# Sparse stages: u by features ahead of v, and the pooling's running sums as shifted additions on GpSimd

## The reference, cut to what matters

```python
POOL_WINDOWS = (2, 4, 8, 16)
def pool_mixer(u, w_pool, pool_scale):
    ug = u.reshape(B, S, N_POOL_GROUPS, POOL_GROUP)          # 4 groups of 128 features
    cs = jnp.cumsum(ug.astype(jnp.float32), axis=1)
    for g, w in enumerate(POOL_WINDOWS):
        c = cs[:, :, g]
        lagged = jnp.pad(c, ((0, 0), (w, 0), (0, 0)))[:, :S]
        cnt = jnp.minimum(t + 1, w).astype(jnp.float32)[None, :, None]
        outs.append((c - lagged) / cnt - ug[:, :, g].astype(jnp.float32))
    d = jnp.stack(outs, axis=2).astype(u.dtype)
    y = jnp.einsum('bsgc,gcd->bsgd', d, w_pool)
    return y.reshape(B, S, POOL_WIDTH) * pool_scale
```

## Time and profile before

| what | value |
| --- | --- |
| median of 3 runs | 1811.44 us (1811.19 to 1811.59) |
| profiled execution | 1811.9 us, of which the span of the profile is 1810.1 us |
| busy in the span | PE 1798.3 us (99%), DVE 1312.2 (72%), ACT 1052.0 (58%), POOL 237.4 (13%) |
| granted clock of PE | 0.999 of full on average |
| the two sparse stages' middles | from about 1256 and from about 1536 us on, the same instructions at the same distances |

### The profile page before, as it was taken

The page is one execution under the profiler, slowest core; times in us unless marked ns, Lnnn a source line. Parts: engine busy times, 40 slices in busy tenths (PEclk is TensorE's granted clock), DMA queues, the critical chain, the costliest instruction groups (busy, mean ns, idle before and its releaser), DMA issues.

```text
span 1810.1 us, 26703 instructions
## 1 busy us (share of the span) xinstructions
PE 1798.3 (99%) x10311; PEld 1546.9 (85%) x10311; DVE 1312.2 (72%) x1714; ACT 1052.0 (58%) x1524; POOL 237.4 (13%) x259
## 2 busy tenths in 40 slices
PE   9999999999999999999999999999999999999998
PEld 7888899788888888889987888889888889888887
DVE  7767778876766776677688677667887667797665
ACT  7555546755655565455476665555775555675443
POOL 2010122110000011003021000002100111301110
PEclk9999999999999999999999999999999999999999
DMA  9686663462765567666345456555447664645662
GB/s 337 219 297 208 172 191 106 140 221 93 252 193 183 163 219 254 228 169 220 118 139 198 136 189 210 188 177 186 154 146 226 190 198 157 230 136 187 196 191 71
DMA packets 226815, 338.96 MB, mean 187 GB/s; under 512 B 22566, under 2 KB 170176, under 8 KB 226432
## 3 DMA queue, kind: packets, MB, share of 16 engines
q1 hardware_dynamic: 219200, 308.11, 52.5%
q0 software_dynamic: 7488, 29.14, 4.8%
HBM read 336.18 MB, written 1.05 MB: 186 GB/s over the span
## 4 chain that ended last, share of the span: by engine, by line
PE 95%; DVE 2%; DMA 1%; ACT 1%; SPq 0%; issue 0%; POOL 0%; DVEq 0%; ACTq 0%
PE ps L1809 92%; PE ps L1814 3%; DVE wlo L1195 1%; DMA raw<-ffn_w_down 1%; DVE xn L1195 1%; ACT whi L742 0%; DVE xs L1203 0%; DVE ahl L1195 0%; SPq L537 0%; POOL region L564 0%; SPq L549 0%; ACT xn L742 0%; DVE region L1195 0%; SPq L541 0%; ACT ahl L742 0%
## 5 line engine op out<-in xcount | busy, mean ns | idle before, releaser
L1195 DVE TENSOR_TENSOR wlo<-raw,whi 128x1024 fp32r<-128x1024 f32 (+2 forms) x452 | 560.7, 1241 | 172.3 <-ACT whi L742 137.2
L742 ACT ACTIVATE whi<-raw 128x1024 fp32r<-128x1024 f32 (+2 forms) x452 | 475.7, 1052 | 74.7 <-PE ps L1809 28.2
L1809 PE MATMUL ps<-ahl,whi 128*128 128x512 f32 (+1 forms) x1824 | 402.7, 355 | 0.6 <-ACT whi L742 0.6
L1809 PEld LDWEIGHTS ps<-ahl,whi 128*128 128x128 f32 x1824 | 320.9, 189 | 47.4 <-ACT whi L742 1.0
L742 ACT ACTIVATE region<-ps 128x512 f32<-128x512 f32 (+2 forms) x268 | 155.9, 582 | 272.9 <-PE ps L1809 220.2
L1809 PE MATMUL ps<-whi,ahl 128*128 128x512 f32 (+2 forms) x944 | 299.0, 385 | 0.5 <-ACT whi L742 0.5
L1809 PE MATMUL ps<-ahl,wlo 128*128 128x256 f32 x1520 | 244.4, 283 | 0.0
L1809 PEld LDWEIGHTS ps<-ahl,wlo 128*128 128x128 f32 x1520 | 214.8, 191 | 6.4
L1809 PEld LDWEIGHTS ps<-whi,ahl 128*128 128x128 f32 x944 | 174.2, 188 | 34.7 <-ACT region L742 1.6
L1195 DVE TENSOR_TENSOR mlo<-raw,mhi 128x1024 fp32r<-128x1024 f32 (+2 forms) x132 | 163.3, 1237 | 44.8 <-ACT mhi L742 35.4
L1809 PE MATMUL ps<-whi,hhi 128*128 128x512 f32 x472 | 185.7, 393 | 0.0
(11 more groups left out here) (176 smaller groups left out, 2349.1 us busy)
## 6 DMA issues: line engine op xcount, KB each, us to landing
raw<-w_ff SPq DMA_DIRECT2D x64, 1024.0 KB, 5.4
raw<-ffn_w_down SPq DMA_DIRECT2D x44, 1024.0 KB, 5.0
raw<-ffn_w_up SPq DMA_DIRECT2D x40, 1024.0 KB, 5.7
raw<-ffn_w_gate SPq DMA_DIRECT2D x39, 1024.0 KB, 5.3
raw<-w_in SPq DMA_DIRECT2D x34, 1024.0 KB, 5.4
raw<-w_out SPq DMA_DIRECT2D x16, 1024.0 KB, 4.9
raw<-xa_wk SPq DMA_DIRECT2D x8, 1024.0 KB, 5.1
raw<-xa_wv SPq DMA_DIRECT2D x8, 1024.0 KB, 5.0
```

Of the source, the lines that this page charges most:

```text
L742: e.activation(o, i, f, **kw).then_inc(*act.did(*names))
L1195: e.tensor_tensor(o, a, b, op).then_inc(*dve.did(*names))
L1809: m = e.matmul(o, l, r, start=start, stop=stop)
```

## The change

Per sparse stage:

- u is multiplied the other way round (`up`: features on the partitions, tokens as 256 columns), in two pieces of 256 features, ahead of v instead of behind it. It goes to PSUM banks 0 and 1, and v to banks 2 and 3, where u was. It is no longer scaled by ACT's per-partition scale; `turn_scales` on PE and `scales` on ACT make the roots as a row `R2S`, and POOL multiplies u by it.
- POOL adds shifted copies of u along the row (window 2, then 4, 8, 16 from one another), with 16 cleared elements ahead of each row; it corrects the first 16 tokens with the small constant `c_fix`, which takes the place of `c_pool`. ACT scales the four sums by 1/w in place, POOL subtracts u (`lagged`), which gives `DT`.
- PE's products with the matrix and ACT's copies of them go. PE's `pooled(0)` moves behind `out_part(0, 0)`, next to `pooled(1)`, and both wait for both `lagged`.
- The names in `take` swap u and v; the pieces' places in the queues stay.

```diff
-            for tag, c0, n in (("q", 512, 512), ("k", 1024, 512), ("v", 1536, 512), ("u", 0, 512)):
+            for tag, c0 in (("q", 512), ("k", 1024), ("u", 0), ("v", 1536)):
                 for c in range(2):
-                    item(s, tag, rows(wi, 4 * c, 4 * c + 4, c0, c0 + n), 4, n)
+                    if tag == "u":
+                        item(s, tag, rows(wi, 0, 8, 256 * c, 256 * c + 256), 8, 256)
+                    else:
+                        item(s, tag, rows(wi, 4 * c, 4 * c + 4, c0, c0 + 512), 4, 512)
...
+        UA, SB = [x.rearrange("p (g n) -> p g n", g=4) for x in (XN[:, 576:1664], R[:, 8704:9792])]
+        SCV = R[:, 4352:5168].rearrange("p (g n) -> p g n", g=3)
+        SUMS = (SB[:, 0, 16:272], SCV[:, 0, 16:272], SB[:, 2, 16:272], SCV[:, 2, 16:272])
... (gpsimd, sparse)
-                e.dma_start(PM, A["c_pool"]).then_inc(*region_in.did(("pool", l)))
+                e.dma_start(R[:, 9792:9856], A["c_fix"]).then_inc(*region_in.did(("pool", l)))
...
                 q.wait_ge(*pe.at("a_turned", s, 1, 1))
+                for v in (UA, SB, SCV):
+                    q.wait_ge(*pool.last())
+                    e.memset(v[:, :, 0:16], 0.0).then_inc(*pool.did())
                 q.wait_ge(*act.at("iq_rest", l, 1))
                 rope(iqh[:, :, 0:9, :], 9)
...
                 rope(kn.rearrange("p (m h d) -> p m h d", m=2, h=8), 8, ("k_rope", l))
+                for c in range(2):
+                    q.wait_ge(*act.at("u", l, c))
+                    u = UA[:, 2 * c:2 * c + 2, 16:272]
+                    tt(u, u, bm(R2S, 2), ALU.mult)
+                tt(SB[:, :, 16:272], UA[:, :, 16:272], UA[:, :, 15:271], ALU.add)
+                tt(SCV[:, :, 16:272], SB[:, 1:4, 16:272], SB[:, 1:4, 14:270], ALU.add)
+                tt(SB[:, 2:4, 16:272], SCV[:, 1:3, 16:272], SCV[:, 1:3, 12:268], ALU.add)
+                tt(SCV[:, 2, 16:272], SB[:, 3, 16:272], SB[:, 3, 8:264], ALU.add)
+                q.wait_ge(*region_in.at("pool", l))
+                for a, v in enumerate((SB, SCV)):
+                    tt(v[:, 0::2, 16:32], v[:, 0::2, 16:32], FIX[:, a], ALU.mult, ("sums", l, a))
+                q.wait_ge(*dve.at("score", l, 1))
+                for a, v in enumerate((SB, SCV)):
+                    q.wait_ge(*act.at("means", l, a + 2))
+                    tt(DTV[:, a::2, :], v[:, 0::2, 16:272], UA[:, a::2, 16:272], ALU.subtract, ("lagged", l, a))
... (scalar, sparse)
                 natural((2, 3), qn, "q")
+                scales(s)
                 heads(iqT, 4, "iqT")
...
                 heads(sqT, 2, "sqT")
-                take(s, "v", 1)
+                take(s, "u", 1)
+                pool_input(0)
                 heads(skT, 2, "skT")
-                take(s, "u", 0)
-                natural((0, 1), V, "v")
+                take(s, "v", 0)
+                pool_input(1)
                 exps("s", l, 0, 128, sP, 1.0)
                 exps("s", l, 1, 128, sP, 1.0)
-                take(s, "u", 1)
+                take(s, "v", 1)
                 take(s, "w_out2", 0)
-                natural((2, 3), U, "u")
+                natural((2, 3), V, "v")
                 turned(0)
                 turned(1)
-                means(0)
                 halves(s + 0.5, 0, 1, SVALUE[0])
-                means(1)
+                means()
                 pooled(0)
                 exps("s", l, 2, 256, sP, 1.0)
                 pooled(1)
...
+                def means():
+                    for g in (0, 2, 1, 3):
+                        q.wait_ge(*pool.at("sums", l, g % 2))
+                        put(SUMS[g], SUMS[g], ACT.Copy, ("means", l, g), scale=1.0 / POOL_WINDOWS[g])
... (tensor, sparse)
                 natural(s, "q", (2, 3), 512, ("q", l))
+                turn_scales(s)
...
-                natural_part(s, "v", 0, (0, 1), 512)
+                up(s, "u", 0, 0, ("u", l, 0))
...
-                natural_part(s, "v", 1, (0, 1), 512, ("v", l))
+                up(s, "u", 1, 1, ("u", l, 1))
...
                 scores(1)
-                natural_part(s, "u", 0, (2, 3), 512)
-                natural_part(s, "u", 1, (2, 3), 512, ("u", l))
+                natural_part(s, "v", 0, (2, 3), 512)
+                natural_part(s, "v", 1, (2, 3), 512, ("v", l))
...
+                q.wait_ge(*act.at("u", l, 1))
+                scores(3)
                 q.wait_ge(*act.at("v", l))
-                scores(3)
-                q.wait_ge(*act.at("u", l))
-                q.wait_ge(*region_in.at("pool", l))
-                for a in range(2):
-                    if a:
-                        values(0)
-                        values(1)
-                        q.wait_ge(*dve.at("s_shift", l, 2, 1))
-                    for g in (2 * a, 2 * a + 1):
-                        (two products of U with PM for each group: means)
+                values(0)
+                values(1)
                 def pooled(a):
-                    q.wait_ge(*act.at("means", l, a))
+                    q.wait_ge(*pool.at("lagged", l, 1))
...
-                pooled(0)
                 q.wait_ge(*dve.at("a", s + 0.5, 0, 1))
                 out_part(0, 0, first=True)
+                pooled(0)
                 pooled(1)
```

More of the change, by code:

```diff
@@ L124, in constants @@
     ).astype(np.float32)
-    pm = []
-    for w in POOL_WINDOWS:
-        cnt = np.minimum(t + 1, w)[:, None]
-        m = np.where((dist >= 0) & (dist < w), 1.0 / cnt, 0.0) - np.eye(T)
-        m = m.T
-        pm.append(np.concatenate([m[0:128, :], m[128:256, 128:256]], axis=1))
-    pool = np.concatenate(pm, axis=1).astype(np.float32)
-    return {"c_small": small, "c_decay": decay, "c_pool": pool}
+    fix = [[w / np.minimum(np.arange(16) + 1, w) for w in POOL_WINDOWS[a::2]] for a in range(2)]
+    fix = np.broadcast_to(np.asarray(fix).reshape(1, 64), (128, 64)).astype(np.float32)
+    return {"c_small": small, "c_decay": decay, "c_fix": np.ascontiguousarray(fix)}
 def bc(ap, n):
@@ L333, in build @@
         R2F, R2H, R2M = [R[:, c:c + 256] for c in (9216, 3840, 7168)]
-        R2 = {"ffn": R2F, "relu": R2F, "hybrid": R2H, "memory": R2M}
+        R2S = XN[:, 1664:1920]
+        R2 = {"ffn": R2F, "relu": R2F, "hybrid": R2H, "memory": R2M, "sparse": R2S}
         R2V = R2F.unsqueeze(1).broadcast_to([128, 2, 256])
@@ L437, in build @@
         V = R[:, 3328:4352]
-        U = R[:, 4352:5376]
+        UA, SB = [x.rearrange("p (g n) -> p g n", g=4) for x in (XN[:, 576:1664], R[:, 8704:9792])]
+        SCV = R[:, 4352:5168].rearrange("p (g n) -> p g n", g=3)
+        FIX = R[:, 9792:9856].rearrange("p (a g n) -> p a g n", a=2, g=2)
+        SUMS = (SB[:, 0, 16:272], SCV[:, 0, 16:272], SB[:, 2, 16:272], SCV[:, 2, 16:272])
         ikT = R[:, 5376:5632]
@@ L446, in build @@
         DT = R[:, 11136:12160]
+        DTV = DT.rearrange("p (g n) -> p g n", g=4)
         sP = [R[:, 1024 * i:1024 * i + 1024].rearrange("p (h n) -> p h n", h=4) for i in range(2)]
@@ L454, in build @@
         SBANK, STURN, SVALUE = (4, 6, 6, 0), ((4,), (5,), (2, 3), (2, 3)), (4, 4, 0, 1)
-        MEANBANK, POOLBANK = (3, 6), (2, 3)
+        POOLBANK = (2, 3)
         cosv = COS.rearrange("p (m j) -> p m j", m=2)
@@ L1134, in sparse @@
                 index(0)
-                take(s, "v", 0)
+                take(s, "u", 0)
                 natural((0, 1), kn, "k")
@@ L1139, in sparse, with pool_input @@
                 heads(sqT, 2, "sqT")
-                take(s, "v", 1)
+                take(s, "u", 1)
+                def pool_input(c):
+                    q.wait_ge(*pe.at("u", l, c))
+                    put(UA[:, 2 * c:2 * c + 2, 16:272], PS[:, c, :].rearrange("p (g n) -> p g n", g=2), ACT.Copy, ("u", l, c))
+                pool_input(0)
                 heads(skT, 2, "skT")
-                take(s, "u", 0)
-                natural((0, 1), V, "v")
+                take(s, "v", 0)
+                pool_input(1)
                 exps("s", l, 0, 128, sP, 1.0)
                 exps("s", l, 1, 128, sP, 1.0)
-                take(s, "u", 1)
+                take(s, "v", 1)
                 take(s, "w_out2", 0)
-                natural((2, 3), U, "u")
+                natural((2, 3), V, "v")
                 turned(0)
                 turned(1)
-                def means(a):
-                    q.wait_ge(*pe.at("means", l, a))
-                    put(DT[:, a * 512:a * 512 + 512], PS[:, MEANBANK[a], :], ACT.Copy, ("means", l, a))
+                def means():
+                    for g in (0, 2, 1, 3):
+                        q.wait_ge(*pool.at("sums", l, g % 2))
+                        put(SUMS[g], SUMS[g], ACT.Copy, ("means", l, g), scale=1.0 / POOL_WINDOWS[g])
                 def pooled(a):
```

5 lines of the change are left out of this document (removed).

## The result

The changed kernel takes 1828.59 us (median of 4 runs, 1828.01 to 1829.52) against 1811.51 us (4 runs, 1811.19 to 1811.73) for the kernel before on the same chip: ratio 1.0094, 95% interval [1.0081, 1.0107]. It is 17 us slower; the forecast was 1828. The span of the profiled execution grew from 1810.1 to 1826.8 us, by 16.7.

What follows compares the result with a forecast made beforehand. PE, busy 99% of the span, was taken as the bound, with DVE within 0.4 us at out_part(0, 0). Per stage 4.55 + 2.35 + 1.2 = 8.1 us, two stages 16.2, gave 1828 us; range 1817 to 1834.

Steps and rivals of the forecast that it cites:

- PE and DVE reach `out_part(0, 0)` together, so PE's removed work is worth 0.3 us: At out_part(0, 0), PE and DVE arrive within 0.4 us, so removing 2.9 us of PE work wins only 0.3 per stage.
- The faster rival: PE's removed 2.9 us per stage less 0.84 would count at out_part(0, 0), giving 1807.3 us; chance 0.07.
- `scores(0)` 0.84 later, DVE 0.96: Ahead of the heads: u's narrower products and turn_scales delay scores(0) by 0.84 us; DVE then runs 0.96 late.
- Holds of the two small operations, 2.0 + 0.1 = 2.1: POOL's additions hold DVE's two 128x4 operations at the maxima through the shared port, 2.1 us per stage, bounds 0 and 3.7.
- `lagged` against the split, 1.7: POOL's two subtractions hold DVE's split ahead of the heads' low half by 1.7 us per stage, lower value 1.1.
- +4.55: Predicted delay in us of the start of out_part(0, 0) per stage, from DVE's late start and the holds.
- `pooled(0)` behind `out_part(0, 0)`, +2.35: From out_part(0, 0) to turn_scores(2), the moved products delay ACT's and DVE's queues: 2.35 us per stage, lower bound 0.87.
- The clock, 1.2 out of 0 to 2.7: PE's 7 us gap may drop its clock, slowing out_part(0, 0): 1.2 us per stage, between 0 and 2.7.
- The no-hold rival: POOL's instructions do not hold DVE's; each stage loses 3.1 us, giving 1817.6 us; chance 0.23.
- the no-change rival: Moved pooled(0) costs little and holds are zero, only 0.84 + 0.87 per stage: 1814.8 us; chance 0.06.
- the long low clock: Clock stays low over both pooled and out_part(1, 0) too, 5 us per stage: 1836 us; chance 0.06.
- The signs named ahead: Profile: shift(0) 0.9 later, 2 us 128x4 operation, split over 3.5, PE idle 7, low clock, turn_scores(2) waiting for DVE's pooled.

Runs made afterwards that it cites:

- e5: The kernel before without the eight products with the running-sum matrix per sparse stage, ACT's copies reading u instead: 1812.79 us against 1811.79.
- e1: The changed kernel with POOL's product for the second half of u and its additions held until DVE has the maxima of unit 1: 1820.98 us.
- e8: The kernel before with idle POOL work in scratch: a clear, and five additions from the end of scores(0) on: 1815.80 us.
- e2: The changed kernel with POOL's two subtractions waiting for DVE's low halves of the heads: 1826.18 us.
- e3: The changed kernel with twelve unread float32 products of 256 columns behind values(1), in PE's idle stretch: 1824.55 us.
- e10: The kernel before with only PE's four products pooled(0) moved behind out_part(0, 0): 1816.33 us.
- e9: The changed kernel with e1's delay, ACT's exponentials before pooled(0), seven idle products, POOL's first product later, DVE's split before pooled(0), half a u piece later: 1818.02 us.
- e12: The changed kernel with POOL's products behind maximum(0) and maximum(1), DVE's pooled(0) between split halves, half a u piece later, four idle products: 1813.04 us.

## Why the forecast was right, step by step

*PE and DVE reach `out_part(0, 0)` together, so PE's removed work is worth 0.3 us.* Shown by e5: 0.33 in the heads' distance, of which 0.22 is waited away again in stage 10, and nothing in the time. The faster rival, which needed this work to count, is out.

*`scores(0)` 0.84 later, DVE 0.96.* Measured 0.77 (1585.55 for 1576.88, less 7.90) and 0.77 (1586.31 for 1577.64).

*Holds of the two small operations, 2.0 + 0.1 = 2.1.* Measured 1.50 + 0.75 = 2.25: the sum was right, its parts by luck, since the forecast had the addition begin half a microsecond before DVE's operation and end on 2.4 us, and it took 1.90. That the cause is POOL is shown from both sides, by e1 (holds gone) and e8 (holds made in the kernel before). The rule that the Trainium skill gives in SBUF — State Buffer, that the shared pair of ports is held for a whole instruction, agrees with the trace: 1587.95 to 1589.62 against POOL's end at 1589.59. The same page of the Trainium skill, section "Who interferes with whom", also says that `tensor_reduce` never contends on this chip; the trace agrees, with 0.69 us beside POOL's additions and without them.

*`lagged` against the split, 1.7.* Measured 0.96, under the lower bound of 1.1: only one of the split's two instructions was held. The first had begun 0.15 us before POOL's first subtraction and held that; the second was held in turn, 2.18 us for 1.24. e2 shows what the hold is worth.

With DVE's 0.38 us to spare these give 0.77 + 2.25 + 0.96 = 3.98 for the low half of the heads, and +3.65 for `out_part(0, 0)`; the forecast had +4.55.

*`pooled(0)` behind `out_part(0, 0)`, +2.35.* Measured +2.6 (tails of e1, e3 and e10 in stage 10, 11.69 to 11.70, against 9.10). The chain of ACT, exponentials, reciprocal and split was as told, but the place where PE waits was not: the forecast had PE wait for DVE's `pooled(1)` ahead of `turn_scores(2)`. It waits earlier, ahead of `out_part(2, 0)`, for the first half of the split that stands behind the reciprocal. The sum came out near because both hang on the same instruction of DVE.

*The clock, 1.2 out of 0 to 2.7.* Measured 2.54 in stage 10 and 2.01 in stage 8 (e3). This is the term that was mis-sized most. The row at 1806 us was the right precedent for the fall; the value taken was low. The forecast also read the span's first products (0.22 us for 128 columns) as the low level, but the granted clock there is 1.00 (0 to 4 us of the kernel before), so that row does not show it; the kernel after does, with 1.28 us for three products of 512 columns at 0.50 against 0.69 at 1.00. By the rule of the Trainium skill that the forecast named there (TensorE: Matmul & The Clock Gate, Part 1) the loss would be nearer 2.7 than 0, and both stages agree.

The sum: stage 10 lost 3.65 + 2.60 + 2.54 = 8.79. Stage 8 lost 0.77 ahead of `scores(0)`, 2.95 in the heads and 4.61 in the tail, 8.33. Together 17.12, against 17.08 by the medians; the span grew by 16.7 only, as the profile after comes to stage 8 0.43 us early. Forecast 8.1 each, 16.2. In stage 10 a term too large by 0.9 met two too small by 1.3 and 0.25, so the hit is better than its parts, and that is luck; the mechanisms, and that each has about this weight, are not. The no-hold rival (1817.6) is refuted by the rows and e1, the no-change rival by e10 alone, the long low clock by the windows, where the clock is full again within `pooled`.

The signs named ahead came, most of them somewhat smaller (`shift(0)` 0.77 later, a 128x4 operation of 1.67 us, a split of 3.44, an idle stretch of 6.12), but one: `turn_scores(2)` does not wait for DVE's `pooled`. Open: what decides whether the clock falls behind a given short gap (last section).

## What to carry to other kernels

Before moving work to GpSimd, list what VectorE does in SBUF in the stretch where it will run. Here `tensor_scalar`, `tensor_tensor` and `scalar_tensor_tensor` with their inputs in SBUF were held to the end of one of GpSimd's instructions, a 0.17 us one as well as one half of a 2.5 us split. The rounds of maxima (0.43 and 0.41 us), the reciprocals (0.18), the reductions (0.69) and the operations that read PSUM (0.88 for two) kept their lengths beside GpSimd's additions. Shifting the work by a microsecond can pick another victim (e9), and laying it beside the instructions that are not held can free it (e12). Where two queues reach a point within some tenths of each other, work taken from one is worth those tenths; ask what the other does there first. When a few products are moved back on one engine, follow who evicts them and what is queued behind the eviction: here four products of 0.2 us cost 2.6 us per stage through an ACT queue, a DVE queue and a weight piece that had nothing to do with them.
